# Two value products a block on a stationary operand that holds the high and the low part side by side

## What is computed

```python
# retention, chunks of 128 tokens
scores = jnp.einsum('bnihd,bnjhd->bnhij', qc, kc) * decay
inner = jnp.einsum('bnhij,bnjhe->bnihe', scores, vc)
...
o = (inner + cross).reshape(B, S, H, Dh)
mu = jnp.mean(o, axis=-1, keepdims=True)
var = jnp.mean(jnp.square(o - mu), axis=-1, keepdims=True)
return (o - mu) * lax.rsqrt(var + 1e-5)

# stick-breaking attention
log_fail = jnp.where(before, jax.nn.log_sigmoid(-z), 0.0)
later = lax.cumsum(log_fail, axis=3, reverse=True) - log_fail
log_a = jax.nn.log_sigmoid(z) + later
a = jnp.where(before, jnp.exp(jnp.where(before, log_a, 0.0)), 0.0)
return jnp.einsum('bhqk,bhkd->bhqd', a.astype(v.dtype), v)
```

## Time and profile before

| | us |
|---|---|
| median of 3 runs | 1502.76 |
| lowest and highest | 1500.36, 1503.28 |
| span of the profiled execution | 1500.5 |
| PE busy | 1452.3 |
| DVE busy | 828.7 |
| ACT busy | 683.7 |
| POOL busy | 201.9 |

### The profile page before, as it was taken

How to read it: one execution, slowest core, us unless ns; L and a number is a source line. 1 busy time by engine, 2 the same in 40 slices (tenths; PEclk the granted TensorE clock), 3 DMA queues, 4 the chain that set the end, 5 groups by cost and what they waited for, 6 DMA issues and landing times.

```text
span 1500.5 us, 22048 instructions
## 1 busy us (share of the span) xinstructions
PE 1452.3 (97%) x8524; PEld 1226.9 (82%) x8524; DVE 828.7 (55%) x1455; ACT 683.7 (46%) x1302; POOL 201.9 (13%) x319
## 2 busy tenths in 40 slices
PE   7999999899999999999999999989999999999997
PEld 4887876678988888888998777769988888888996
DVE  6678646776645444432275577574754444422474
ACT  4565536676542222221363556676532232321563
POOL 0000000443310000000130222451300000000221
PEclk9999999999999999999999999999999999999999
DMA  9542440004033333333404211503133333332321
GB/s 365 197 167 85 124 157 10 1 2 169 2 99 98 98 98 98 94 95 94 152 3 167 71 57 43 169 16 99 33 109 98 94 92 96 103 105 92 120 85 56
DMA packets 42148, 146.71 MB, mean 98 GB/s; under 512 B 4673, under 2 KB 7121, under 8 KB 41682
## 3 DMA queue, kind: packets, MB, share of 16 engines
q1 hardware_dynamic: 37986, 128.99, 27.2%
q0 software_dynamic: 3072, 15.71, 2.8%
q10 hardware_dynamic: 1008, 0.89, 0.2%
HBM read 141.39 MB, written 4.19 MB: 97 GB/s over the span
## 4 chain that ended last, share of the span: by engine, by line
PE 84%; DVE 9%; ACT 3%; issue 2%; DMA 1%; POOL 0%; DVEq 0%; SPq 0%; ACTq 0%; POOLq 0%
PE B L285 22%; PE B L287 22%; PE B L286 22%; PE CROW_P L285 3%; PE CROW_P L287 3%; PE CROW_P L286 3%; PE B L1789 2%; PE B L2025 1%; DVE AL L1381 1%; DVE WADA L1143 1%; PE CROW_P L1868 1%; ACT T L622 1%; PE CROW_P L1768 1%; ACT AH L622 1%; DVE WL L1110 1%
## 5 line engine op out<-in xcount | busy, mean ns | idle before, releaser
L285 PE MATMUL B<-UH,WH 128*128 128x512 f32 (+1 forms) x1008 | 374.7, 372 | 4.6 <-DVE WL L1110 3.7
L287 PE MATMUL B<-UH,WL 128*128 128x512 f32 (+1 forms) x1008 | 372.3, 369 | 0.0
L286 PE MATMUL B<-UL,WH 128*128 128x512 f32 (+1 forms) x1008 | 372.3, 369 | 0.0
L622 ACT ACTIVATE WH<-RAW 128x1024 fp32r<-128x1024 f32 x174 | 182.6, 1052 | 120.0 <-DMA RAW<-in_stream 111.6
L285 PEld LDWEIGHTS B<-UH,WH 128*128 128x128 f32 x1008 | 190.4, 189 | 38.0 <-issue 5.0
L286 PEld LDWEIGHTS B<-UL,WH 128*128 128x128 f32 x1008 | 190.3, 189 | 32.0
L287 PEld LDWEIGHTS B<-UH,WL 128*128 128x128 f32 x1008 | 190.2, 189 | 32.0
L1110 DVE TENSOR_TENSOR WL<-RAW,WH 128x1024 fp32r<-128x1024 f32 x94 | 116.0, 1240 | 143.8 <-ACT WH L622 143.7
L1462 DVE TENSOR_TENSOR WL<-RAW,WH 128x1024 fp32r<-128x1024 f32 x80 | 98.0, 1226 | 76.7 <-ACT WH L622 73.9
L622 ACT ACTIVATE T<-B 128x256 f32<-128x256 f32 (+5 forms) x186 | 86.5, 465 | 109.9 <-PE B L287 63.3
L622 ACT ACTIVATE T<-T 128x512 f32<-128x512 f32 (+3 forms) x131 | 68.7, 525 | 130.8 <-DVE T L1466 119.2
(11 more groups left out here) (419 smaller groups left out, 3146.2 us busy)
## 6 DMA issues: line engine op xcount, KB each, us to landing
RAW<-in_stream SPq DMA_DIRECT2D x202, 512.0 KB, 3.7
WADA<-in_w_ada SPq DMA_DIRECT2D x8, 1024.0 KB, 16.7
RAW<-in_stream SPq DMA_DIRECT2D x16, 384.0 KB, 3.5
WADA<-in_w_ada SPq DMA_DIRECT2D x2, 2048.0 KB, 11.5
W<-in_w POOLq DMA_DIRECT2D x2, 2048.0 KB, 12.1
X<-in_x SPq DMA_DIRECT2D x2, 1024.0 KB, 11.0
DECAY<-in_decay POOLq DMA_DIRECT2D x1, 2048.0 KB, 9.6
X<-in_x POOLq DMA_DIRECT2D x2, 1024.0 KB, 8.2
```

The costliest lines, as they stand in the source:

```text
L285: nc.tensor.matmul(out, lh, rh, start=start, stop=False, **kw)
L286: nc.tensor.matmul(out, lh, rl, start=False, stop=False, **kw)
L287: return nc.tensor.matmul(out, ll, rh, start=False, stop=stop, **kw)
L622: return nc.scalar.activation(out, in_, func, **kw)
```

## The change

- The values of both attentions are kept as `VR` and `VA`, 128 keys by head by two halves by 64 columns: the high and the low part of a head lie side by side. ACT and DVE write them through a strided view (`by_head`), with the same number of elements.
- A block's value product is two matmuls. The first has both halves as its stationary operand, 128 columns, and the high weights as its moving operand: rows 0 to 63 of the bank collect high by high, rows 64 to 127 low by high. The second has the high half, 64 columns, and the low weights.
- When a head is complete, ACT copies rows 0 to 63 as before, and DVE adds rows 64 to 127: `gn_add` (8 adds of 64x512 in the retention) and `sb_head_sum` (8 in the stick-breaking attention). Whoever waited for the copy (`gn_x`, `SBN["y"]`) now waits for the add (`gn_a`, `sb_ya`).
- In the retention the first matmul of a block waits only for the high weights and the second for the low ones, and in steps 5 to 12 `compress_hidden` stands ahead of the value products.
- The square of a pair of heads moves from `head_out` to the end of ACT's step n (`sb_head_square`).
- `VBH` and `VBL` get another shape with the same layout.

```diff
-        VRH, VRL = hb("VRH", 32, [P, 4, SEQ], F32R), hb("VRL", 40, [P, 4, SEQ], F32R)
+        VR = hb("VR", 32, [P, 4, NH, 2, HD], F32R)
...
+            def sb_head_square(p):
+                wait(act, E["sb_ya"], 2 * p + 2)
+                wait(act, SBN["sum"], p - 1)
+                SBN["sq"].mark(f(SQA[:, SQ_SLOT[SBN["y"]][p], :], YA[:, p, :], ACT.Square))
...
+            def gn_add(p):
+                for s in range(2):
+                    wait(dve, E["gn_x"], 2 * p + s + 1)
+                    rows = pair_rows(s)
+                    E["gn_a"].mark(tt(T[10][rows, :], T[10][rows, :], B[s][HD:P, :], ALU.add))
+
             dve.wait_ge(decay_here, 16)
             for m in range(18):
+                if m in (6, 10, 14):
+                    gn_add((m - 6) // 4)
                 if m in (8, 12, 16):
                     gn_g((m - 8) // 4)
...
                 if m == 0:
+                    gn_add(3)
                     compressed_keys_values()
...
+            def sb_head_sum(h):
+                wait(dve, SBN["y"], h + 1)
+                rows, p = pair_rows(h), h // 2
+                E["sb_ya"].mark(tt(YA[rows, p, :], YA[rows, p, :], B[h % 2][HD:P, :], ALU.add))
...
                 if 0 <= n - 3 < 32:
                     sb_weights_lo(n - 3)
+                if n >= 11 and n % 8 in (3, 4):
+                    sb_head_sum(2 * ((n - 11) // 8) + n % 8 - 3)
                 if 0 <= n - 1 < 32:
                     sb_soft_lo(n - 1)
...
-                        wait(pe, E["ret_lo"], u + 1)
-                        wait(pe, E["gn_x"], 2 * p - 1 + s)
-                        E["ret_pv"].mark(mm3(B[s][0:HD, kj * P:], VRH[:, kj, o], VRL[:, kj, o],
-                                             AH[:, u % 4, 0:L], AL[:, u % 4, 0:L], kj == 0, kj == 3))
...
+                        wait(pe, E["ret_hi"], u + 1)
+                        wait(pe, E["gn_a"], 2 * p - 1 + s)
+                        mat(B[s][:, kj * P:], VR[:, kj, 2 * p + s, :, :], AH[:, u % 4, 0:L], start=kj == 0, stop=False, skip_group_check=True)
+                        wait(pe, E["ret_lo"], u + 1)
+                        E["ret_pv"].mark(mat(B[s][0:HD, kj * P:], VR[:, kj, 2 * p + s, 0, :], AL[:, u % 4, 0:L],
+                                             start=False, stop=kj == 3, skip_group_check=True))
...
-                wait(pe, SBN["y"], h - 1)
+                wait(pe, E["sb_ya"], h - 1)
                 wait(pe, E["p5_vlo"], max(4 - kj, u + 1) if u < 2 else 4 - kj)
-                E["sb_pv"].mark(mm3(B[h % 2][0:HD, kj * P:], VAH[:, kj, o], VAL[:, kj, o],
-                                    AHS[:, u % 4, 0:sb_len(u)], ALS[:, u % 4, 0:sb_len(u)], kj == 3, kj == 0,
-                                    skip_group_check=True))
+                mat(B[h % 2][:, kj * P:], VA[:, kj, h, :, :], AHS[:, u % 4, 0:sb_len(u)], start=kj == 3, stop=False, skip_group_check=True)
+                E["sb_pv"].mark(mat(B[h % 2][0:HD, kj * P:], VA[:, kj, h, 0, :], ALS[:, u % 4, 0:sb_len(u)],
+                                    start=False, stop=kj == 0, skip_group_check=True))
```

57 lines of the change are left out of this document (30 added, 27 removed).

## The result

The changed kernel takes 1508.88 us in the median of 4 runs (1508.73 to 1514.56), the kernel before 1502.77 (1500.36 to 1503.28). The ratio is 1.0051, 95% interval 1.0031 to 1.0070: slower, by about 6 us. All medians here are of executions at a mean granted clock of 0.98 or more; one of the run e13 took 2390.7 us at 0.555 and is left out. The profiled execution of the changed kernel has a span of 1507.0 us against 1500.5.

A forecast was written before the change was run, and what follows sets the result against it. Bound by PE mostly, by a DVE and ACT chain at the retention's end, in parts of stick-breaking and at the banded start. Retention -0.1 and stick-breaking +0.8 make +0.7; 1500.5 + 0.7 + 2.3 = 1503.5 us, range 1498.5 to 1506.5.

The forecast's parts named there:

- What it removes: Both attentions: 64 matmuls, the third product of each block, worth 9.3 us of PE time, half in each.
- What the wide stationary costs: First products: a 128-column weight load exposed by 0.05 us behind short matmuls; 1.5 us in stick-breaking, 1.2 in the retention.
- Retention up to step 13: Dense PE: 2.0 us gained, adds of pairs 0 and 1 hidden behind `compress_hidden`, else 0.6 us a pair.
- Retention, the end: From step 13 DVE has no idle time: the new pair of adds costs 1.2 us, PE's savings gain 0.
- The additions: Retention's adds on DVE: third pair 1.2 us at its end, last pair 0.7 us at the sparse attention's start.
- Stick-breaking, the gain: Stick-breaking: of 3.1 us saved on PE, 1.7 lost where other engines set the pace, 1.4 kept.
- Stick-breaking, the adds: Stick-breaking loop: adds lengthen it by 0.6 us where it has no room; cost 1.1 us, bounds 0 and 2.4.
- Start of the banded attention: First banded steps: adds of heads 6 and 7 delay ACT; cost 1.1 us, bounds 0.5 and 1.3.
- The strided copies into `VR` and `VA`: Copies of the values in both attentions: same number of elements as before, no cost.
- Rival B: End of the retention: PE's wait grows to about 2.3 us and the clock falls; +2.9, 1506.4 us; chance 0.15.
- Rival A: Both attentions: adds are hidden and PE keeps 3.1 + 2.2 us, giving 1497.5 us; chance 0.20.

The follow-up runs named there:

- e13: The kernel before, with the retention's Silu replaced by a plain copy, both table loads around it gone and one load put in step 9: 1503.21 us.
- e8: The kernel before, with stick-breaking's third value product left out, 64-column operands kept and no additions: 1501.06 us.
- e6: The kernel before, with the change in stick-breaking alone and its eight additions left out: 1500.81 us.
- e9: The kernel before, with the change in retention alone, additions kept, value products ahead of the compression as before: 1503.99 us.
- e5: The kernel before, with the change in retention alone, old order of value products and compression, its eight additions left out: 1500.24 us.
- e4: The kernel before, with only the order changed: compression ahead of the value products in retention steps 5 to 12: 1505.69 us.
- e2: The kernel before, with the change in retention alone, new order and additions included: 1506.09 us.
- e1: The changed kernel, with only the order undone: value products ahead of the compression again in retention steps 5 to 12: 1508.18 us.
- e14: e9 with the Silu replaced by a plain copy, both table loads around it gone and one load put in step 9: 1504.93 us.
- e12: e2 with PE's wait in retention step 14 filled with 13 products into a free bank: 1506.20 us.
- e3: The kernel before, with the change in stick-breaking alone, additions included: 1505.38 us.
- e15: The kernel before, with two products and additions in the first two pairs of heads of the retention only, old order: 1501.26 us.
- e7: e3 with each addition placed last in VectorE's step: 1504.72 us.
- e17: e14 with casts of zeros moved earlier on VectorE, of which only one left its busy stretch: 1503.89 us.

## Why the prediction was wrong

The prediction was 1503.5 us with a range up to 1506.5, and "slower" at 0.21; measured are 1508.9. By its steps:

- **What it removes.** Right where rows show it. The page has 2.0 us less PE work where the terms give 9.3 - 2.7 = 6.6; PE's busy time also holds products at half the clock, so this difference isn't read further.
- **What the wide stationary costs.** Right in the single case (0.05 us). Too large in the sum: 1.5 us was put down for stick-breaking, 0.4 is what e8 gained on e6 up to step 18. For the single load I had weighed a sentence of the Trainium skill (page "TensorE: Matmul & The Clock Gate", section "Architectural detail: the array is 16× 32×32, not 1× 128×128"), that a matmul can begin before its weight load is complete. It says when a matmul can begin and not what it then costs, and my reading of it, that the term would be near 0, isn't borne out: the load was exposed by 0.05 us.
- **Retention up to step 13.** Foretold -2.0, found -1.8 in the changed kernel (-1.6 from its first scores on) and -2.6 without additions. Right. With the old order, so without the cover that I named, the additions of pairs 0 and 1 cost some 0.3 us each (e9 against e5), half of what I had put. What they cost under the cover no run shows.
- **Retention, the end: the step that failed first.** I read that `compress_hidden` now stands ahead of the value products, counted it as cover for the additions, and did not ask who waits for those value products. ACT does: the high parts have four places (`AH[:, u % 4]`), and a new one must wait for the value product of two steps before. Behind it stand the table loads, the Silu and the copies. That costs 3.0 us alone (e4), 2.1 with two products (e2 less e9), and the sum had 0 for it. The fall of the clock on PE is in these figures; of the trace's 12.35 us at the end of the retention 1.35 are the order's and 1.25 the clock's.
- **The additions, the second failure, one of size.** I priced the third pair at 1.2 and the last at 0.7 us. The right mechanism was there (VectorE without a gap), but a pair takes 1.44 us with nothing beside it, and all four pairs are exposed, the first two by 0.3 us each: 3.8 us (e5 and e9) against 1.9. "VectorE without a gap" held only with the old order and a clock of 1.00 (e1); in the changed kernel it waits 1.37 us for the copies and 0.34 and 0.99 us behind them.
- **Stick-breaking, the gain.** Foretold 1.4 kept, measured 1.9. Right.
- **Stick-breaking, the adds.** 1.1 us with a bound of 2.4; measured 3.3. The loop is what I said it is: VectorE's maximum is 0.97 us later in step 20, and POOL, ACT and PE behind it. The term that was mis-sized is that of steps 19 and 20: 0.4 foretold, since the square out of ACT's way should give most of it back, 1.65 found. The square's new place gave little of it back there, and an addition lengthened the loop by 0.97 us in step 20, not by 0.6. Steps 27 and 28 cost 0.9 against 0.7, steps 11 and 12 0.4 against nothing.
- **Start of the banded attention.** 1.1 foretold, 1.3 measured. Right, and by the path named.
- **The strided copies into `VR` and `VA`.** No cost, as foretold: 0.60 and 0.68 us on ACT and 0.69 and 0.75 on VectorE, before and after.
- **Rival B**, the clock. By the sign that I gave for it (below 1.00 between 243 and 257 us) it came true, behind a wait of 3.63 us and not of 2.3; the order had made the wait longer, but in e9 and e14 the clock fell behind 2.28 us as well. B's price of 2.9 us isn't confirmed: the trace has 1.25 us of it at the last low part, and with the clock held there the time stayed (e12).
- **Rival A** had the gain nearly right and the cover wrong: without additions and with the old order the two attentions win 2.4 + 1.9 = 4.3 us of its 5.3.

The account by medians: retention -2.4 (products) +3.8 (additions) +2.1 (order); stick-breaking -1.9 +3.3 +1.3; sum +6.2, measured +6.1. The terms of each attention add up to e2 and e3 by the way they are taken; what is tested is that e2 and e3 add up to the whole.

Two things stay open. One is what share of the median's loss is the granted clock's, since it falls in some executions only; the 1.25 us are from one trace. The other is that e13 and e14 were 0.8 and 0.9 us above their partners (the kernel before and e9) although work was taken away; the intervals overlap, and no row explains it.

## What to carry to other kernels

When a step is moved past another on one engine, list who waits for the step that is now later, on every engine, before pricing what the move covers. The longest wait in a stretch need not be the one that sets its end: take it away in thought and look whether the busiest other engine has a gap; if it has none, as VectorE here, each new operation there costs its whole length. Here, trading a product on the full engine for an operation on an engine at 55% paid only where that engine had room, in the first half of the retention (e15).

## What the runs showed of the hardware

The granted clock falls in some executions and not in others after the same waits. At the first steps of the retention PE waits 0.73 and then 0.90 us in the kernel before and in e7, with the same instructions up to there, and yet the windows from 205 to 212 us read, first before, then e7 (which is 1.65 us later here):

```profile
205.00:212.00 7.00, 6.11 (x41) 3.86 (x42) 6.07 (x16) 3.44 (x8) 0.00 (x0) 1.00 1.00 425
```

```profile
205.00:212.00 7.00, 5.55 (x23) 3.28 (x22) 5.46 (x14) 2.89 (x6) 0.00 (x0) 0.58 1.04 432
```

e7 lost 2.4 us there (offset +1.65 to +4.03). Over all runs the mean granted clock goes with the time: beside e1 to e4 the kernel before took 1500.5 to 1504.1 us at 0.990 to 0.994 and 1504.9 to 1506.7 at 0.987 or 0.988. A difference under 2 us is less than this spread. After a wait of 2.28 us at the copies the clock fell in e9 and e14 and stayed at 1.00 in e1 and e17; after 2.77 (e4), 3.62 (e2) and 3.63 us (the changed kernel) it fell. An addition of 64 x 512 that reads one bank takes 0.69 us, as long as 128 x 512, so using half the partitions saved nothing.
